# Post-norm weight on GpSimd, one DVE operation for scale and residual, transposes a tile sooner, attention output units 2 and 3 in turns

## What is computed

```
def rms_norm(x, g):
    y = x * lax.rsqrt(jnp.mean(x * x, axis=-1, keepdims=True) + EPS)
    return y * g

for i in range(DEPTH):
    h = rms_norm(x, norm_mix_pre[i])
    m = chunked_gmlp(h, ...) if i % 2 == 0 else stick_breaking_attention(h, ...)
    x = x + rms_norm(m, norm_mix_post[i])
    h = rms_norm(x, norm_ffn_pre[i])
    f = jnp.square(jax.nn.relu(h @ w1[i])) @ w2[i]
    x = x + rms_norm(f, norm_ffn_post[i])
```

## Time and profile before

| | us |
|---|---|
| three runs | 2648.39, 2646.04, 2649.50 |
| the profiled execution, its own time | 2653.23 |
| span of its trace | 2651.5 |
| PE busy | 2534.1 (96%) |
| DVE busy | 1482.2 (56%) |
| GpSimd (POOL) busy | 1107.4 (42%) |
| ACT busy | 1031.4 (39%) |

### The profile page before, as it was taken

The page is one execution under the profiler, slowest core; times in us unless marked ns, Lnnn a source line. Parts: engine busy times, 40 slices in busy tenths (PEclk is TensorE's granted clock), DMA queues, the critical chain, the costliest instruction groups (busy, mean ns, idle before and its releaser), DMA issues.

```text
span 2651.5 us, 35475 instructions
## 1 busy us (share of the span) xinstructions
PE 2534.1 (96%) x13100; PEld 2150.5 (81%) x13100; DVE 1482.2 (56%) x1959; ACT 1031.4 (39%) x1507; POOL 1107.4 (42%) x716
## 2 busy tenths in 40 slices
...
GB/s 167 88 86 111 48 64 80 63 93 91 162 150 153 149 240 153 144 159 157 129 96 143 190 88 143 113 109 103 64 74 90 175 155 151 197 208 161 141 165 114
DMA packets 180417, 342.56 MB, mean 129 GB/s; under 512 B 12224, under 2 KB 95168, under 8 KB 178240
## 3 DMA queue, kind: packets, MB, share of 16 engines
...
## 4 chain that ended last, share of the span: by engine, by line
PE 79%; DVE 8%; ACT 4%; issue 4%; DMA 3%; POOL 2%; SPq 0%; DVEq 0%; ACTq 0%; POOLq 0%
PE psum L1143 22%; PE psum L1189 17%; PE psum L960 13%; PE psum L947 12%; PE psum L971 5%; PE psum L1279 3%; PE psum L1266 2%; PE psum L1249 2%; DVE stick L2157 1%; PE psum L1064 1%; DMA a_raw<-a_forms 1%; ACT brk L1663 1%; DVE ra_lo L2037 1%; POOL rw_lo L901 1%; DVE acc L1756 1%
## 5 line engine op out<-in xcount | busy, mean ns | idle before, releaser
L1189 PE MATMUL psum<-rw_hi,ra_hi 128*128 128x512 f32 x896 | 353.1, 394 | 19.7 <-DVE acc L2055 16.1
L1189 PE MATMUL psum<-rw_lo,ra_hi 128*128 128x512 f32 x896 | 351.5, 392 | 0.0
L1189 PE MATMUL psum<-rw_hi,ra_lo 128*128 128x512 f32 x896 | 351.1, 392 | 0.0
L814 POOL TENSOR_TENSOR w_lo<-stage,w_hi 128x1024 fp32r<-128x1024 f32 x56 | 134.1, 2415 | 504.6 <-ACT w_hi L1342 504.6
L901 POOL TENSOR_TENSOR rw_lo<-blk,rw_hi 128x512 fp32r<-128x512 f32 x152 | 232.6, 1560 | 184.3 <-ACT rw_hi L1492 184.3
L2157 DVE TENSOR_TENSOR_SCAN stick<-psum,brk 128x128 f32<-128x128 f32 (+7 forms) x128 | 172.6, 1354 | 125.6 <-ACT psum L1669 125.2
L2037 DVE TENSOR_TENSOR ra_lo<-a_raw,ra_hi 128x512 fp32r<-128x512 f32 x224 | 227.6, 1024 | 23.2 <-ACT ra_hi L1481 23.2
L1481 ACT ACTIVATE ra_hi<-a_raw 128x2048 fp32r<-128x2048 f32 x56 | 107.4, 1917 | 341.7 <-PE psum L1189 229.1
L920 POOL TENSOR_TENSOR brk<-brk,stick 128x128 f32<-128x128 f32 (+7 forms) x128 | 152.9, 1205 | 190.0 <-DVE stick L2157 177.4
L960 PE MATMUL psum<-w_hi,hT_hi 128*128 128x256 f32 x768 | 219.8, 286 | 1.4 <-DVE hT_lo L2164 1.4
L960 PE MATMUL psum<-w_lo,hT_hi 128*128 128x256 f32 x768 | 218.8, 285 | 0.0
...
## 6 DMA issues: line engine op xcount, KB each, us to landing
...
```

The source lines that it names most:

```text
L814: pool.tensor_tensor(w[b][1][:, c], raw[:, c], w[b][0][:, c].bitcast(F32), ALU.subtract).then_inc(unit_ready, 1)
L1189: mm = pe.matmul(psum[:, down_bank(n, tp), :], ring_a[n % 3][sa][:, k, tp * P:(tp + 1) * P], ring_w[n % 3][sw][:, k, :], start=(p in (1, 2 ...
```

## The change

- **Who does what.** Step 3 and 4 are cut anew for all tiles of all boundaries. GpSimd multiplies the tile by the weight, `gain_m`: `acc = acc * gpost` (L834 of the changed kernel), as soon as `square_m(t)` has read the tile. DVE then does scale and residual in one operation (L1759): `xt = acc * rstd + xt`. `add_x`, L1739 and L1743 are gone.
- **Order.** On DVE `pre_norm(t-1)` stands where `pre_norm(t-2)` stood. On ACT `square_x(t)` stands behind `square_m(t)`, where `square_x(t-1)` stood. The transposes of tile t-2 stand where those of t-3 stood, in the boundaries with an up-projection (1 and 3).
- **GpSimd.** S2 and S4 are formed with S1, ahead of the tiles. `h_forms` is cut into two halves of two operations each, with `gain_m(6)` or `gain_m(7)` between them. The splits of the first two weight forms stand behind `gain_m(6)` in both layers.
- **PE.** The products (0,2), (1,1) and (1,2) stand behind some of the transposes they stood ahead of.
- **Attention output.** Units 2 and 3 are taken in turns: (2,0) (2,1) (3,0) (2,2) (3,1) (2,3) (3,2) ... (2,7) (3,6) (3,7).

The core of the diff:

```diff
+O_TURNS = [(2, 0), (2, 1)] + [x for t in range(NT - 2) for x in ((3, t), (2, t + 2))] + [(3, NT - 2), (3, NT - 1)]
...
-            def add_x(b, t0=0, t1=6):
+            def gain_m(b, t0, t1):
                 for t in range(t0, t1):
-                    pool.wait_ge(post, post_steps(b, t))
-                    pool.wait_ge(x_in[t % 4], 16 * (2 * b + t // 4 + 1))
-                    pool.tensor_tensor(xt[t % 4][:], acc[:, t, :], xt[t % 4][:], ALU.add).then_inc(x_add, 1)
+                    if t == 0:
+                        pool.wait_ge(g_in, 16 * (1 + 2 * (b - 1) + 2) if b < 4 else 16 * 8)
+                    pool.wait_ge(m_sq, NT * (b - 1) + t + 1)
+                    pool.tensor_tensor(acc[:, t, :], acc[:, t, :], gpost[:], ALU.mult).then_inc(m_gain, 1)
...
             def mlp_boundary(b, layer):
                 w_forms(layer)
-                if layer:
-                    up_split(layer, 0, 1)
-                    up_split(layer, 0, 2)
-                add_x(b)
+                gain_m(b, 0, 6)
                 h_forms(b, layer, 0)
-                if not layer:
-                    up_split(layer, 0, 1)
-                    up_split(layer, 0, 2)
+                gain_m(b, 6, 7)
+                h_forms_rest(b, layer, 0)
+                up_split(layer, 0, 1)
+                up_split(layer, 0, 2)
                 h_forms(b, layer, 1)
+                gain_m(b, 7, NT)
+                h_forms_rest(b, layer, 1)
...
@@ ACT, boundary(b) @@
                     if b < 4:
                         if t >= 3:
                             take_hi(b, t - 3)
-                        if t:
-                            square_x(b, t - 1)
+                        square_x(b, t)
...
@@ DVE @@
             def post_norm(b, t):
                 dve.wait_ge(m_rt, n + 1)
                 dve.reciprocal(rstd[:, 0, t:t + 1], rt[:, 0, t:t + 1]).then_inc(post, 1)
-                dve.scalar_tensor_tensor(acc[:, t, :], acc[:, t, :], rstd[:, 0, t:t + 1], gpost[:], ALU.mult, ALU.mult).then_inc(post, 1)
-                if t >= 6:
-                    dve.tensor_tensor(xt[t % 4][:], acc[:, t, :], xt[t % 4][:], ALU.add).then_inc(post, 1)
+                dve.wait_ge(m_gain, n + 1)
+                dve.scalar_tensor_tensor(xt[t % 4][:], acc[:, t, :], rstd[:, 0, t:t + 1], xt[t % 4][:], ALU.mult, ALU.add).then_inc(post, 1)
...
             def boundary(b, finish):
                 for t in range(NT):
                     finish(t)
-                    if b < 4 and t >= 2:
-                        pre_norm(b, t - 2)
-                    post_norm(b, t)
+                    if b < 4 and t:
+                        pre_norm(b, t - 1)
                     if b < 4 and t >= 3:
                         take_lo(b, t - 3)
+                    post_norm(b, t)
```

More of the change, by code:

```diff
@@ L166, in down_before, with o_bank @@
     return max([m for m in range(k) if same(*DOWN[m]) == same(*x)], default=None)
+O_TURNS = [(2, 0), (2, 1)] + [x for t in range(NT - 2) for x in ((3, t), (2, t + 2))] + [(3, NT - 2), (3, NT - 1)]
+O_ORDER = [(u, t) for u in (0, 1) for t in range(NT)] + O_TURNS
+O_AT = places(O_ORDER)
+O_FREE = FI_O + O_AT[(2, NT - 1)] + 1
+def o_bank(u, t):
+    return t % 4 if u < 2 else 4 + 2 * (u - 2) + t % 2
 def finishes(t):
@@ L932, in _ @@
             mlp_boundary(3, 1)
-            add_x(4, 0, 2)
+            gain_m(4, 0, 2)
             down_w_split(1, STEPS - 1)
-            add_x(4, 2)
+            gain_m(4, 2, NT)
         @block.tensor
@@ L1319, in _ @@
             pe.wait_ge(stick_done, HEADS * NT)
-            for u in range(D // UC):
-                ready(U_O + u)
-                last = u == D // UC - 1
-                for t in range(NT):
-                    before = 3 if not last or t < 2 else 1
-                    n_item(DVE_EV, FI_O + u * NT + t, t % (2 if last else 4), u % 2, t, before).then_inc(front_psum, 1)
-                    if last and 3 <= t <= 6:
-                        if t == 3:
-                            pe.wait_ge(dve_evac, FI_END - NT - FI_V2)
-                        quad(3, 1, 1, t - 3)
-                        quad(3, 1, 2, t - 3)
-            pe.wait_ge(dve_evac, FI_END - FI_V2)
+            for u, t in O_ORDER:
+                if t == 0:
+                    ready(U_O + u)
+                if u < 2:
+                    held = O_AT[(u, t)] - 4
+                else:
+                    held = O_AT[(u, t - 2)] if t >= 2 else None
+                if held is not None and held >= 0:
+                    pe.wait_ge(dve_evac, FI_O - FI_V2 + held + 1)
+                n_item(None, None, o_bank(u, t), u % 2, t, None).then_inc(front_psum, 1)
+                if u == 3 and 2 <= t <= 5:
+                    if t == 2:
+                        pe.wait_ge(dve_evac, FI_O - FI_V2 + 2 * NT)
+                    quad(3, 1, 1, t - 2)
+                    quad(3, 1, 2, t - 2)
             mlp_up(3, 1)
```

165 lines of the change are left out of this document (93 added, 72 removed).

## The result

The changed kernel takes 2684.88 us (median of 4 runs, 2681.95 to 2688.96), the kernel before 2648.94 us beside it (4 runs): ratio 1.0135, 95% interval 1.0122 to 1.0147, slower. The forecast was 2671, range 2654 to 2685: the sign and the places were right, the size was 14 us short. 2684.88 lies 0.12 us inside the end of the range, and outside the 2660 to 2680 that the forecast thought most likely.

What follows compares the result with a forecast made beforehand. PE was busy 96% of the span, its boundary waits bound by the relay ACT, DVE, GpSimd, ACT, DVE. Boundaries 1 to 4 at +5, +10.5, -4 and +11.5 gave +23 on 2648.4: 2671 us, range 2654 to 2685.

Steps and rivals of the forecast that it cites:

- the relay: All boundaries: ACT, DVE, GpSimd, ACT, DVE in turn; square to scale grows from 1.71 to 3.63 us per tile.
- the ring: Boundaries 1 to 3: ACT's new order closes a loop of square, gain, scale and residual, square of x: 6.65 us a tile.
- rw_hi of step 27: Boundary 2: the high part of step 27, behind the ring, comes at 1246.3 in place of 1240.66, +5.6 us.
- (25,2): Boundaries 2 and 4: a product that must wait for (24,2)'s bank to be emptied, new PE waits of 4.8 and 3.6 us.
- Boundary 4's tail: Last two tiles of boundary 4: 1.9 us more each, less the two saved additions' 2.5, so +1.4.
- I take 2: Boundary 4: clock cost after new waits, two exposed products, 0 to 4.7 us, taken as 2 within the +11.5.
- Clock: 0 to 3; I take 1.2: Boundary 2: cost of a lowered PE clock, taken as 1.2 us within the +10.5.
- about 30: Boundary 1: first product to steady stream shrinks from 36.6 us to about 30, four of ten waits covered, two transposes done.
- 29 to 32: Boundary 3: first product to steady stream, 34.8 us before, takes 29 to 32, the clock low at first.
- (c): Rival: gain meets pre-norms and forms more often, every new wait lowers the clock; 2684 us, chance 15%.
- (b): Rival, no change: the gain is nearer DVE's 1.23 us than 2.40 and the clock costs nothing; 2650 us, chance 6%.
- (a): Rival, faster: PE has work during the relay, boundary 3 -14, boundary 1 -12, 2 and 4 at +18; 2640 us, chance 6%.

Runs made afterwards that it cites:

- combo: Changed kernel with weight and residual on DVE in boundaries 1 and 3, the earlier kernel's division and orders in 2 and 4: 2639.35 us, 0.9958 of the kernel before.
- forms_late: Changed kernel with weight forms S2 and S4 back behind the tiles and the old places of S2 and S3: 2683.72 us, 1.0128 of the kernel before.
- dve_all: Changed kernel with weight-and-scale and residual as two DVE operations, none on GpSimd, low-part splits behind them: 2654.38 us, 1.0018 of the kernel before.

## Why the prediction was right, and where its size was off

**Right.** The sign, and where and through whom PE comes to wait. That the total still lies inside the range is luck, by 0.12 us: single runs of the changed kernel go from 2681.95 to 2688.96, and the four boundaries together cost 16.8 us more than their four terms. The gain stands on the relay, 2.40 us where nothing meets it, 3.8 us from square to scale; the ring of 6.65 (6.70); the ends of all main waits; rw_hi of step 27, forecast +5.6, came 13.3 later in time and 5.7 later against the first square. (25,2) waits 5.01 and 5.03 (4.8 and 3.6 forecast). Boundary 4's tail, +1.4: from the end of the last product to the end 10.2 us before and 11.6 after. First product of boundary 3, 63.2 and 63.9 us behind unit 1's last copy, by a wait of 10.24 (9 to 10 forecast).

**Mis-sized, term by term.** In each of the four boundaries the clock is the larger part of the miss. I had put it at 2 us in boundary 4, at 1.2 in 2, at "low at first" in 3 and at nothing in 1.

- *Boundary 4, "I take 2" of 0 to 4.7.* PE's busy time rose by 4.5. Three waits of 5.03, 4.93 and 3.60 us stand where one of 3.83 stood; behind each of the last two the next 24 matmuls took 8.3 us. In boundary 2 of the kernel before 24 took 8.56 behind the wait of 6.82, and later 24 took 5.46. The bound of 4.7 was low by its own rows: they differ by 3.1, and two exposed products make 6.2. Idle time rose by 11.1 in place of 9.5. Sum +15.6 for +11.5.
- *Boundary 2, "Clock: 0 to 3; I take 1.2".* Busy +3.1, idle +10.2 (9.3 forecast): +13.3 for +10.5. In the chain of waits of the changed kernel, the 24 matmuls behind its two longest waits there (8.72 and 5.46 us):

```profile
1275.40 7.95 PE psum L1208 x24
1296.03 7.90 PE psum L1208 x24
```

- *Boundaries 1 and 3, from the first product to the stream, "about 30" and "29 to 32".* The first products came where forecast (12.5 us later against the first square in boundary 1, 11.3 forecast). The stretch behind them took 33.2 and 35.8. The run without the weight has the same instructions and the same two waits there in boundary 1 (3.72 and 3.46 us; here 3.79 and 3.46) and took 30.6, and 32.1 in boundary 3. The difference is the clock: in boundary 1 PE is idle for 9.0 us of the stretch in both, and busy for 24.2 at a clock of 0.85 against 21.7 at 0.94. Changed kernel, then the one without the weight:

```profile
638.15:671.36 33.21, 24.20 (x120) 19.61 (x121) 25.25 (x31) 14.07 (x27) 19.46 (x11) 0.85 0.14 48
```

```profile
616.10:646.72 30.62, 21.66 (x120) 17.66 (x121) 27.08 (x33) 15.28 (x30) 17.17 (x10) 0.94 0.15 52
```

Windows over single products of 12 matmuls, the changed kernel:

```profile
661.16:666.31 5.15, 5.15 (x16) 4.05 (x15) 1.01 (x2) 0.60 (x1) 0.00 (x0) 0.55 0.00 0
2015.26:2020.72 5.46, 5.46 (x13) 4.24 (x14) 1.01 (x2) 0.35 (x2) 5.38 (x4) 0.50 0.00 0
```

and the same two products without the weight:

```profile
638.68:641.67 2.99, 2.99 (x17) 2.45 (x16) 1.35 (x3) 0.60 (x1) 0.00 (x0) 1.00 0.00 0
1973.39:1976.38 2.99, 2.99 (x14) 2.45 (x15) 1.74 (x4) 1.99 (x4) 2.99 (x2) 1.00 0.90 289
```

At 1973.39 PE had stood 1.13 us, at 2015.26 10.24: 2.99 and 5.46 us, 1.00 and 0.50 of 2.4 GHz. Boundary 1 +9.2 for +5, boundary 3 +1.7 for -4. The reason given for the shorter stretch, covered waits, failed as well: PE's idle time in it was 7.6 us before and is 9.0 in boundary 1, and 7.9 before and after in boundary 3. What shrank in boundary 1 is busy time, 29.0 to 24.2 us, with fewer instructions left (128 and 120) and a clock of 0.78 and 0.85. About 30 us was met without the weight, with as much idle time, so that number was luck.

Of the 16.8 us that the four sums are short, the clock is about 10.7: 2.5 and 1.9 in boundaries 4 and 2 (busy time less what was taken for it), 2.6 and 3.7 in 1 and 3 (the stretch less that without the weight, which had the same waits in boundary 1; in boundary 3, 3.08 and 3.81 for 3.11 and 3.79). The rest, 6, is split over all four. The 4.1 us by which the changed kernel's other stretches are shorter lie within their scatter and belong to no term: in seven of the ten other runs, too, these stretches are 2.7 to 5.2 us shorter in sum than in this one execution of the kernel before.

**The rivals.** (c), "every new wait lowers the clock", said 2684 and named this cause, beside longer meetings of gain and pre-norm, which are there too (19 of 32 gains took 2.60 us or more); the mechanism of the forecast and the size of (c) are what happened. By it the MLP boundaries lose 8 us more than forecast and the others 5; they lost 6.9 and 9.9 more. I gave it 15% and took both clock terms that have bounds below the middle of them, though the earlier trace rows show 8.56 against 5.46 us for 24 matmuls behind one such wait. (b) falls: no gain took less than 2.34. (a) falls for this kernel, but its first half can be had: without the gain boundaries 1 and 3 give 14 us each, where (a) had 12 and 14.

**What I had not seen.** The forecast took gain and orders for two losses to be added. They interact: in boundary 1 new orders alone +15.4, gain alone +18.0, both +9.2, and new orders with neither operation on the relay -14.2. A part of it is which operations stand in series in a tile's loop: 8.56 us, 7.47 (from tile 4 on), 6.70 and 6.1.

The period doesn't decide alone. combo has 6.68 us a tile in boundary 1, as good as the changed kernel's 6.70, and gives -2.7 for +9.2. Its tiles start sooner. GpSimd and DVE of the changed kernel, up to the first scale, and DVE's first scale in combo:

```profile
585.96 1.26 POOL L850 TENSOR_TENSOR s<-stage 128x512 f32<-128x512 f32 x1 [13.14 <-DMA stage<-mlp_w_in]
...
589.92 2.34 POOL L834 TENSOR_TENSOR acc<-acc,gpost 128x1024 f32<-128x1024 f32 x1
...
592.39 1.29 DVE L1759 SCALAR_TENSOR_TENSOR xt<-acc,rstd,xt 128x1024 f32<-128x1024 f32 x1 [11.98 <-POOL acc L834]
```

```profile
583.35 1.29 DVE L1800 SCALAR_TENSOR_TENSOR acc<-acc,rstd,gpost 128x1024 f32<-128x1024 f32 x1 [3.09 <-DMA gpre<-norm_ffn_pre_in]
```

In the changed kernel the first gain is queued behind three weight forms, the first of which waits for its weights until 585.96; the scale comes 14.9 us behind the first square, in combo 6.1. The forecast had this start right (593.0) and I never tested it as a cause of its own: forms_late moved two of the three forms (12.2 us).

The Trainium skill (GPSIMD Engine Reference, "Engine selection") says to keep two-input elementwise work on the Vector engine. The runs agree as far as the relay goes (dve_all 30 us under the changed kernel), with a limit that they show too: with both operations DVE is busy for 6.53 of 6.68 us a tile in boundary 1 (combo), and the boundary comes in dve_all to -3.1 where it came to -14.2 without the weight.
